# Group norm by nine matmuls after two adds on GpSimd, and the final norm interleaved with the last down product

## The reference, cut to what matters

```
# branch B: the scan's output y (1088 x 2048), gated, then a norm over each of four groups of 512 channels
y  = y * silu(z)
yg = y.reshape(b, L, 4, 512)
yg = yg * rsqrt(mean(yg*yg, axis=-1) + EPS)
y  = yg.reshape(b, L, 2048) * norm_w          # then y @ w_branch_b
...
# the end: feed-forward, residual add, final norm
f = (silu(h2 @ w_gate) * (h2 @ w_up)) @ w_down # 1024 -> 2816 -> 1024
x = x + gate2 * f
y = rmsnorm(x) * final_norm_w
```

## Time and profile before

| | us |
|---|---|
| median of three runs (2466.42 to 2469.03) | 2466.65 |
| profiled execution | 2464.14 |
| its span in the trace | 2462.2 |
| mean granted TensorE clock | 0.963 |

### The profile page before, as it was taken

The page is one execution under the profiler, slowest core; times in us unless marked ns, Lnnn a source line. Parts: engine busy times, 40 slices in busy tenths (PEclk is TensorE's granted clock), DMA queues, the critical chain, the costliest instruction groups (busy, mean ns, idle before and its releaser), DMA issues.

```text
span 2462.2 us, 36426 instructions
## 1 busy us (share of the span) xinstructions
PE 2318.4 (94%) x13835; PEld 2230.6 (91%) x13835; DVE 1238.7 (50%) x1939; ACT 604.8 (25%) x993; POOL 107.0 (4%) x160
## 2 busy tenths in 40 slices
PE   5999999996999999979998997989999999999995
PEld 4899999996999999879998896889999999999994
DVE  4655455554666766544566545534333444433345
ACT  4211133422333233322111423221111111111111
POOL 1000000000010111001110000010000000000000
PEclk8999999998999999978999998999999999999996
DMA  7455323334565655633323333211111111111104
GB/s 241 124 175 170 106 81 91 94 104 128 162 189 159 187 173 175 187 108 107 99 71 110 116 133 120 90 46 45 43 43 43 43 43 43 43 51 43 43 26 154
DMA packets 319869, 258.77 MB, mean 105 GB/s; under 512 B 13444, under 2 KB 293702, under 8 KB 319808
## 3 DMA queue, kind: packets, MB, share of 16 engines
q1 hardware_dynamic: 263535, 204.11, 27.5%
q10 hardware_dynamic: 52368, 41.57, 5.4%
q0 software_dynamic: 3904, 12.26, 1.4%
HBM read 195.69 MB, written 62.21 MB: 105 GB/s over the span
## 4 chain that ended last, share of the span: by engine, by line
PE 50%; issue 44%; DVE 3%; ACT 1%; POOL 1%; DMA 1%; SPq 0%; ACTq 0%; POOLq 0%; DVEq 0%
PE PS L1008 27%; PE PS L1205 11%; PE PS L1187 2%; PE PS L1255 2%; PE PS L1181 1%; PE PS L1184 1%; PE PS L1085 1%; PE PS L1194 1%; PE PS L1171 1%; PE PS L1072 0%; PE PS L1128 0%; PE PS L1266 0%; DVE pool_s L1743 0%; ACT junk L678 0%; DVE act_a_lo L1703 0%
## 5 line engine op out<-in xcount | busy, mean ns | idle before, releaser
L1008 PE MATMUL PS<-act_a_hi,w_hi 128*128 128x364 f32 (+1 forms) x1296 | 434.6, 335 | 24.1 <-DVE act_a_lo L1703 15.3
L1401 DVE TENSOR_TENSOR w_lo<-w_raw,w_hi 128x1024 fp32r<-128x1024 f32 x156 | 195.6, 1254 | 488.9 <-ACT w_hi L655 487.4
L1008 PE MATMUL PS<-act_a_hi,w_lo 128*128 128x364 f32 (+1 forms) x1296 | 431.4, 333 | 0.0
L1008 PE MATMUL PS<-act_a_lo,w_hi 128*128 128x364 f32 (+1 forms) x1296 | 431.3, 333 | 0.0
L1347 PE MATMUL PS<-act_b_lo,w_hi 128*128 128x364 f32 (+1 forms) x1056 | 347.9, 329 | 0.0
L1347 PE MATMUL PS<-act_b_hi,w_lo 128*128 128x364 f32 (+1 forms) x1056 | 347.7, 329 | 0.0
L1347 PE MATMUL PS<-act_b_hi,w_hi 128*128 128x364 f32 (+1 forms) x1056 | 347.7, 329 | 0.0
L655 ACT ACTIVATE w_hi<-w_raw 128x1024 fp32r<-128x1024 f32 x156 | 164.5, 1055 | 482.2 <-PE PS L1008 215.6
L1008 PEld LDWEIGHTS PS<-act_a_hi,w_hi 128*128 128x128 f32 x1296 | 248.8, 192 | 26.4 <-DVE act_a_lo L1703 16.4
L1008 PEld LDWEIGHTS PS<-act_a_lo,w_hi 128*128 128x128 f32 x1296 | 248.8, 192 | 0.0
L1008 PEld LDWEIGHTS PS<-act_a_hi,w_lo 128*128 128x128 f32 x1296 | 248.2, 192 | 0.0
(11 more groups left out here) (264 smaller groups left out, 3419.2 us busy)
## 6 DMA issues: line engine op xcount, KB each, us to landing
w_raw<-in_w_in SPq DMA_DIRECT2D x64, 512.0 KB, 5.2
acs_in<-acs_c SPq DMA_DIRECT2D x36, 512.0 KB, 5.3
ada<-in_w_ada SPq DMA_DIRECT2D x16, 1024.0 KB, 7.2
gp_s<-gp ACTq DMA_DIRECT2D x24, 544.0 KB, 3.8
w_raw<-in_w_ffn_gate SPq DMA_DIRECT2D x22, 512.0 KB, 3.9
w_raw<-in_w_ffn_up SPq DMA_DIRECT2D x22, 512.0 KB, 3.8
w_raw<-in_w_ffn_down SPq DMA_DIRECT2D x22, 512.0 KB, 3.5
xs_in<-xs_c SPq DMA_DIRECT2D x36, 256.0 KB, 3.1
```

Source lines behind the costliest of these rows:

```text
L1008: e = pe.matmul(PS[:, n, 0:w], wt[a], at_[b][:, o:o + w], start=(k == 0 and q == 0), stop=(k == len(steps) - 1 and q == 2))
L1401: dve.tensor_tensor(w_split[v][1][:, :], w_raw[v][:, :], w_split[v][0][:, :].bitcast(F32), ALU.subtract)\
```

## The change

It has two parts that don't touch each other.

**Branch B's norm.** POOL adds the four square tiles of a group in two instructions (`sum_squares`): tiles 0 and 1 plus tiles 2 and 3 (2176 columns), then tile 0 plus tile 1 (1088). `group_sum` then needs nine matmuls. It also moves. For group 0 it stands inside the scan's last step, ahead of the last third, and VectorE's `group_variance(0)` no longer waits for the scan's last third to be copied; on POOL's queue `tokens_rms(0)` moves ahead of the last state's store. For the next groups it moves from behind unit 0 to the middle of unit 1.

**The last down product** goes by ranges: for each of three ranges all eight output tiles. `turn_out` and `norm3_step` for tiles 0 to 4 stand between its pieces, where the tokens of the tile are complete; tiles 5 to 8 follow. `final_w` and the first two `fr` are loaded when the last gate and up products are done, 24 pieces earlier than before. The loop over the norm's tiles is written out.

```diff
+    TOKENS_AFTER = [-(-min((t + 1) * CH, T) // THIRD) for t in range(NCH)]
+    LAST_STEPS = [(n, f, {(1, 3): 0, (1, 6): 1, (2, 1): 2, (2, 3): 3, (2, 5): 4}.get((n, f)))
+                  for n in range(3) for f in range(KT)]
...
-            sp.wait_ge(mm["ffn"], FFN_SUBS)
+            sp.wait_ge(mm["ffn"], FFN_SUBS - 24)
             sp.dma_start(final_w[:, :, :], A["final_norm_w"].rearrange("(f c) -> f c", c=P).partition_broadcast(P))\
...
+            def sum_squares(g):
+                pool.wait_ge(ysq_ready, 4 * g + 4)
+                pool.tensor_tensor(ysq[:, 0:2, :], ysq[:, 0:2, :], ysq[:, 2:4, :], ALU.add).then_inc(ysum_step, 1)
+                pool.wait_ge(ysum_step, 2 * g + 1)
+                pool.tensor_tensor(ysq[:, 0, :], ysq[:, 0, :], ysq[:, 1, :], ALU.add).then_inc(ysum_step, 1)
...
+                if g == GROUPS - 1:
+                    sum_squares(0)
                 store_state(0, g)
+            tokens_rms(0)
             store_state(1, GROUPS - 1)
...
             for g in range(GROUPS):
+                if g < GROUPS - 1:
+                    sum_squares(g + 1)
                 pool_out(2 * g)
...
                 if c == NCH - 1:
                     state_turn(g, 11)
+                    if not ahead:
+                        pe.wait_ge(v_skip, NCH * GROUPS)
+                        group_sum(0)
                 third_of(b, 2 * k + 1)
+
+            def group_sum(g):
+
+                pe.wait_ge(ysum_step, 2 * g + 2)
+                if g:
+                    pe.wait_ge(rms_vec, 2 * g)
+                for c in range(NCH):
+                    L = CH if c < NCH - 1 else DEC
+                    e = pe.matmul(PS[0:L, 3, c:c + 1], ysq[:, 0, c * CH:c * CH + L], ones[:, 0:1], start=True, stop=True)
+                e.then_inc(gs_mm, 1)
...
-                    if q == 0 and g < GROUPS - 1:
-                        group_sum(g + 1)
+                        if q == 1 and m == 0 and g < GROUPS - 1:
+                            group_sum(g + 1)
...
+            for n, f, t in LAST_STEPS:
+                last_down(n, f)
+                if t is not None:
+                    turn_out(t)
+            for t in range(5, NCH):
+                turn_out(t)
...
+            group_variance(0)
             dve.wait_ge(mm_free["ssd"], 75)
             dve.sem_inc(mm_free["brb"], 3)
-            group_variance(0)
...
+            def norm3_step(t):
+                norm3_add(t)
+                if t:
+                    norm3_scale(t - 1)
+                variance(n3, t, t % 2, CH if t < NCH - 1 else DEC)
+
+            for n, f, t in LAST_STEPS:
+                last_sum(n, f)
+                if t is not None:
+                    if t == 0:
+                        dve.wait_ge(fw_in, 16)
+                    norm3_step(t)
+            for t in range(5, NCH):
+                norm3_step(t)
+            norm3_scale(NCH - 1)
```

More of the change, by code:

```diff
@@ L233, in build @@
     y_back = [S(f"y_landed{i}") for i in range(2)]
-    ysq_ready, gs_mm, rms_vec, rms_pow, rms_wide, yn_ready, yb_hi, yb_lo = [S(n) for n in (
-        "ysq_ready", "group_sum", "group_variance", "group_rms", "rms_spread", "y_normed", "y_hi", "y_lo")]
+    ysq_ready, ysum_step, gs_mm, rms_vec, rms_pow, rms_wide, yn_ready, yb_hi, yb_lo = [S(n) for n in (
+        "ysq_ready", "ysq_summed", "group_sum", "group_variance", "group_rms", "rms_spread", "y_normed", "y_hi", "y_lo")]
     tails_t, tails_v, tails_out = S("tails_turned"), S("tails_copied"), S("tails_stored")
@@ L561, in store_state, with tokens_rms @@
                 pool.dma_start(ssm_out[q][g], state_out[q][:, :, :]).then_inc(edge_store[q], 16)
+            def tokens_rms(g):
+                if g:
+                    pool.wait_ge(rms_wide, g)
+                pool.wait_ge(rms_vec, 2 * g + 2)
+                for r, c in [(P, slice(0, NCH - 1)), (DEC, slice(NCH - 1, NCH))]:
+                    w_ = c.stop - c.start
+                    pool.tensor_tensor(rms_g[0:r, c], rms_v[0:r, c], half[0:r, 0:1].broadcast_to([r, w_]), ALU.pow)\
+                        .then_inc(rms_pow, 1)
+            def sum_squares(g):
[3 more added lines that the diff above has]
+                pool.tensor_tensor(ysq[:, 0, :], ysq[:, 0, :], ysq[:, 1, :], ALU.add).then_inc(ysum_step, 1)
             for g in range(GROUPS):
@@ L990, in norm3_squares @@
                 squares(n3, fx[v][:, :, :], fjunk[:, :, :], v, t, L)
-            act.wait_ge(mm_free["ffn"], FFN_DVE + 3)
             with act.Fori(0, 4) as i:
@@ L1245, in _ @@
             group(GROUPS - 1, True)
[L1247 to L1257, removed]
             def spread_rms(g):
@@ L1268, in spread_rms @@
                 e.then_inc(rms_wide, 1)
-            group_sum(0)
             pe.wait_ge(yg_ready, NCH * GROUPS + 3)
@@ L1382, in _, with last_down, turn_out @@
             pe.wait_ge(f_lo, 2 * FG)
[L1383 to L1388, removed]
+            def last_down(n, f):
+                o, w = SUBS[n]
+                i, v, m = KT * n + f, f // 4, f % 4
+                if i in (0, 4):
+                    unit_ready(U_END - 2 + v)
+                pe.wait_ge(mm_free["ffn"], FFN_DVE - 24 + i + 1)
+                for k in range(2):
+                    for q, (a, b) in enumerate(PASSES):
+                        e = pe.matmul(PS[:, i % 3, 0:w], w_split[v][a][:, k * 512 + m * P:k * 512 + (m + 1) * P],
+                                      f_split[b][:, k, o:o + w], start=(k == 0 and q == 0), stop=(k == 1 and q == 2))
+                e.then_inc(mm["ffn"], 1)
+            def turn_out(t):
                 L = CH if t < NCH - 1 else DEC
+                pe.wait_ge(mm_free["ffn"], FFN_DVE - 24 + 3 + KT * TOKENS_AFTER[t])
                 if t >= 2:
@@ L1937, in _, with last_sum, norm3_add @@
             dve.wait_ge(mm_free["ffn"], FFN_DVE - 24)
-            for v in range(2):
-                sums(v, FFN_SUBS - 24 + 12 * v)
-            def norm3_add(t, v, L=CH):
+            def last_sum(n, f):
+                o, w = SUBS[n]
+                i = KT * n + f
+                dve.wait_ge(mm["ffn"], FFN_SUBS - 24 + i + 1)
+                parts = [(o, w, 0)] if o + w <= SEQ else [(o, SEQ - o, 0), (SEQ, DEC, 1)]
+                for at_, n_, q in parts:
+                    dst = acc[:, f, at_:at_ + n_]
+                    e = dve.scalar_tensor_tensor(dst, PS[:, i % 3, at_ - o:at_ - o + n_], mods[:, GATE2 + f, q:q + 1], dst,
+                                                 ALU.mult, ALU.add)
+                e.then_inc(mm_free["ffn"], 1)
+            def norm3_add(t):
+                v, L = t % 2, CH if t < NCH - 1 else DEC
+                if t >= 2:
+                    dve.wait_ge(n3.scaled, t - 1)
                 dve.wait_ge(n3.landed[v], (t - v) * 8 + 16)
```

21 lines of the change are left out of this document (5 added, 16 removed).

## The result

The changed kernel takes 2427.22 us (median of four runs, 2426.71 to 2428.49), the kernel before in the same comparison 2466.53: a ratio of 0.9842, interval 0.9828 to 0.9855. That is 39.3 us less where 53.4 were forecast. The prediction was 2413, its range 2401 to 2430 holds the time.

A forecast was written before the change was run, and what follows sets the result against it. It took TensorE's chain, with four group sums of 45.33 us together, and the poorly overlapped end as bounds. Gains of 61.3 less 5.5 and 2.4 gave 53.4 us: 2410.7, named as 2413 for the runs' median, range 2401 to 2430.

The forecast's parts named there:

- the stop in branch B: Branch B: POOL's adds stop VectorE's window sums, so evictions come late and TensorE stands; cost 2.4 us, bounds 0 and 7.
- last stage: Last down product and final norm: sharing the time takes 56.8 us in place of 69.1; 12 less, between 14 and 8.
- The sums: Four group sums, scan and branch B: 18 records each in place of 72, 1.65 us each; 38.7 us less.
- The clock behind them: Three products after the later sums: if the clock stays up they fall to 12.06 us each; 5.7 less, bounds 0 and 5.7.
- Variance, power and spread: After the first sum: the wait for variance and power goes, 2.7 us; the spread falls from 4.32 to 2.15, 2.2 less.
- the rival with half clock there: Last stage gains nothing: TensorE idles, its clock falls and matmuls with transposes become the bound again; 2425 us, chance 0.12.
- The stop in the scan: Scan's end: POOL's first add delays VectorE's `y_tok` + `skip` by 4.3 us, plus 1.2 half clock; cost 5.5, bounds 0 and 8.
- 1.2 us of half clock: Scan's end, within the 5.5 us cost: some matmuls expected at half clock after TensorE's long idle.
- The lock costs double: Rival: both adds stop the scan's chain, three branch B groups lose 3 us each, clock falls; 10 more, 2423 us; chance 0.15.

The follow-up runs named there:

- run with held-up evictions: Changed kernel with the square-tile additions on VectorE instead of POOL, in later groups behind a unit's first window sums, ahead of the next evictions; 2417.92 us.
- window_later: Changed kernel with POOL's additions kept and VectorE's window sums and means of branch B one piece of the product later; 2427.06 us.
- the three kernels that kept their evictions in time: Changed kernel without additions, 2404.49 us; the same with sums in thirds, 2403.87; additions on VectorE, in later groups behind the first unit's second-piece evictions, 2405.06.

## Why the prediction came out as it did

The time lies in the range, but the forecast itself was 14 us too fast: the stop in branch B cost seven times what I gave it, and the other terms together gave 2 back. That the time lies inside is in part luck: with a last stage of the 12 forecast it would have been 2430.6.

*The sums (38.7): right.* 45.33 less four of 1.89 is 37.8. *The clock behind them (5.7): right as a term, and given back.* Without additions branch B is 33.9 us shorter; the sums are 27.3 of that, which leaves 6.6. After the change the 36 records behind a sum ran partly at half clock again, through another cause. *Variance, power and spread (2.7 and 2.2): right.* The scan's end without additions is 15.05 shorter, of which the sum is 10.5: 4.6 for the two.

*The last stage (12): 15.4.* The time after the last addition was sized with waits of 0.9 and 1.6 us for loads, and one of 1.80 came; the additions of the third range and the steps were a little shorter than taken; TensorE's clock was 0.89 over the first 15 us, with the slow start, and 1.0 from 2386 to 2405.7, so the rival with half clock there did not occur. That is 1.4 above the upper bound.

*The stop in the scan (5.5, bounds 0 and 8): 6.5,* with 10 to 11 in two other runs. I took the second addition to come after the chain; it stopped the next instruction too, which the upper bound had named: 4.2 us are `y_tok`'s and 2.3 the `state`'s. The 1.2 us of half clock that I had added did come (matmuls near 1046 take 0.51 us, for 0.33 near 1049), but TensorE then still waited 1.15 us for `yg`, so they cost nothing here. The number is closer than its parts.

*The stop in branch B (2.4, bounds 0 and 7): 17.1.* This is the step that failed, in two ways. I wrote that "such an instruction", one with two SBUF operands, stands still, and looked for the window sums. What the additions met first were the copies of 15 columns ahead of them, with one SBUF input. These stand directly behind an eviction and ahead of the next three. The window sums themselves ran undisturbed, 1.33 to 1.34 us each. And I priced the stop as TensorE's waiting time alone: the waits are 8.9 us where the kernel without additions has none; of the other 8.2 some 7.9 are half clock, 4.6 behind the three sums and 3.3 in the pieces ahead of two of them (7.78 and 7.77 for about 6.1). The run with held-up evictions shows both parts of that price without POOL.

In sum 37.8 + 6.6 + 4.6 + 15.4 - 6.5 - 17.1 = 40.8, the table's total. *"The lock costs double"* was the right rival, with the stop of the second addition, the three groups and the clock: it cost three times (23.6 for 7.9), and the last stage paid part of it.

## What to carry to other kernels

Before work goes to an idle engine that can stop a busy one, as POOL did VectorE here, list every instruction of the busy engine that can run in that time, short copies too, and ask for each what is queued behind it: the price is that of the queue. A stop of TensorE is to be priced with the slower matmuls that follow, which here cost about as much as the stop. The same work on the busy engine itself, at a place where nothing urgent stands behind it, cost nothing that could be measured: 2405 us, as without the additions, against 2427.

## What was not expected of the hardware

A copy of 128 x 15 elements took 4.02 us beside an addition of POOL and 2.86 beside a memset, while `y_tok` with its two operands took 0.69 beside a memset. And TensorE's clock did not always fall where it stood, but later: in the run with held-up evictions the first group's sum and the 36 records ahead of it ran at full rate behind a wait of 0.8 us, and those behind the sum took 7.73 us. In `window_later` the second and third sums are followed by 7.68 and 7.72 us, though the product just ahead of the third had run at full rate (18.20 us for 108). No such slow piece followed a later sum in the three kernels that kept their evictions in time (nine sums of nine columns, 6.15 to 6.19 us each). In the seven others with nine columns, all with waits of TensorE, it came behind 17 of 21 later sums. The first sum, in the scan, doesn't follow this: a slow third came behind it in six of the ten traces, among them two of the three kernels that kept their evictions in time (5.71 us, for 4.19 in the third). So a late eviction is not the only way to the half clock behind a sum. Why four later sums were spared, and what decides behind the first one, these runs don't show.
